# Forty modulation units ahead of the projections, forty beside them, and filter blocks in two buffers

## What is computed

```python
# first block
c_act = silu(c)
mod = c_act @ ada_w + ada_b                       # 2048 x 12288
sh1, sc1, g1, sh2, sc2, g2 = split(mod, 6)
h = rmsnorm(x, norm1_g) * (1 + sc1) + sh1
x = x + g1 * token_mixer(h, w_in, ...)            # mixers A, B, C, D: projections, attention, norm, w_out
h = rmsnorm(x, norm2_g) * (1 + sc2) + sh2
x = x + g2 * moe_ffn(h, ...)
# second block: filters, which need nothing of x
h = three layers of sin(fr * (h @ w + b)) on z;  h = (h @ w4) * decay
k = two-sided h;  k = k / sum(abs(k));  k_f = rfft(k)   # kept with hyena_bias added
```

## Time and profile before

| | |
|---|---|
| median of 3 runs | 3142.29 us (3139.79 to 3145.81) |
| the profiled execution, its own time | 3142.81 us |
| its span, first to last instruction | 3141.3 us |
| mean granted TensorE clock | 0.943 |
| PE busy | 2783.9 us (89%) |
| DVE busy | 1893.1 us (60%), 179.1 us of it in 80 modulation units (L886) |
| ACT busy | 1301.0 us (41%) |
| DMA | 645.60 MB, mean 206 GB/s; 564 loads of 1024 KB on SP's queue |

### The profile page before, as it was taken

One profiled execution on the slowest core, in us unless ns is written; L12 is line 12 of the kernel. 1 busy time (PEld: TensorE's weight loads), 2 busy tenths in 40 slices (PEclk: granted clock), 3 DMA queues, 4 the chain that ended last, 5 costly groups with the idle time before them and its releaser, 6 DMA issues.

```text
span 3141.3 us, 42584 instructions
## 1 busy us (share of the span) xinstructions
PE 2783.9 (89%) x16468; PEld 2403.4 (77%) x16468; DVE 1893.1 (60%) x2310; ACT 1301.0 (41%) x1609; POOL 32.1 (1%) x61
## 2 busy tenths in 40 slices
PE   1435999989799999999969898999898999999998
PEld 0112998877678878778759666999787998998996
DVE  7998444345666688889866544354545544545544
ACT  1001444334244457777633133444335543443443
POOL 1000000000000000000000000000000000000000
PEclk9666999889899999999989998999999999999999
DMA  9887534222077779999924333454453555455553
GB/s 368 320 342 305 179 136 161 94 81 108 18 265 248 259 273 357 358 370 375 356 78 180 139 124 132 149 186 174 147 187 141 183 187 192 180 187 189 186 186 122
DMA packets 139360, 645.60 MB, mean 206 GB/s; under 512 B 10286, under 2 KB 10361, under 8 KB 78704
## 3 DMA queue, kind: packets, MB, share of 16 engines
q1 hardware_dynamic: 130656, 593.53, 52.0%
q0 software_dynamic: 6288, 33.76, 3.0%
q10 hardware_dynamic: 2304, 16.78, 1.5%
HBM read 636.64 MB, written 7.39 MB: 205 GB/s over the span
## 4 chain that ended last, share of the span: by engine, by line
PE 73%; DVE 12%; DMA 8%; ACT 3%; issue 3%; DVEq 0%; POOL 0%; ACTq 0%; SPq 0%; POOLq 0%
PE ps L1404 72%; DMA raw<-in_stream 6%; DVE raw L886 3%; DVE w_lo L812 2%; ACT w_hi L503 1%; DMA arena<-in_hyena_bias 1%; PE ps L1487 1%; DMA filters<-arena 1%; DVE arena L942 0%; PE ps L1517 0%; DVE h_lo L861 0%; DMA arena<-in_c_row 0%; DVE arena L869 0%; DVE arena L1324 0%; DVE arena L1322 0%
## 5 line engine op out<-in xcount | busy, mean ns | idle before, releaser
L812 DVE TENSOR_TENSOR w_lo<-raw,w_hi 128x1024 fp32r<-128x1024 f32 x968 | 1171.5, 1224 | 831.7 <-ACT w_hi L503 829.0
L503 ACT ACTIVATE w_hi<-raw 128x1024 fp32r<-128x1024 f32 x968 | 1010.5, 1056 | 784.7 <-PE ps L1404 690.3
L1404 PE MATMUL ps<-h_hi,w_hi 128*128 128x256 f32 x2944 | 842.4, 286 | 26.7 <-DVE h_lo L861 14.5
L1404 PE MATMUL ps<-h_lo,w_hi 128*128 128x256 f32 x2944 | 838.5, 285 | 0.0
L1404 PE MATMUL ps<-h_hi,w_lo 128*128 128x256 f32 x2944 | 838.0, 285 | 0.0
L1404 PEld LDWEIGHTS ps<-h_hi,w_hi 128*128 128x128 f32 x2944 | 571.0, 194 | 28.5 <-issue 28.2
L1404 PEld LDWEIGHTS ps<-h_lo,w_hi 128*128 128x128 f32 x2944 | 571.1, 194 | 0.3
L1404 PEld LDWEIGHTS ps<-h_hi,w_lo 128*128 128x128 f32 x2944 | 570.6, 194 | 0.0
L1404 PE MATMUL ps<-w_hi,r_hi 128*128 128x512 f32 x1184 | 469.0, 396 | 14.4 <-DVE w_lo L812 6.9
L1404 PE MATMUL ps<-w_lo,r_hi 128*128 128x512 f32 x1184 | 462.6, 391 | 0.0
L1404 PE MATMUL ps<-w_hi,r_lo 128*128 128x512 f32 x1184 | 462.5, 391 | 0.0
(11 more groups left out here) (254 smaller groups left out, 1770.3 us busy)
## 6 DMA issues: line engine op xcount, KB each, us to landing
raw<-in_stream SPq DMA_DIRECT2D x564, 1024.0 KB, 4.9
arena<-in_mod_units ACTq DMA_DIRECT2D x16, 1024.0 KB, 4.8
filters<-arena POOLq DMA_DIRECT2D x4, 1280.0 KB, 5.6
arena<-filters POOLq DMA_DIRECT2D x4, 1280.0 KB, 6.2
arena<-in_c_row POOLq DMA_DIRECT2D x2, 1024.0 KB, 10.0
x<-in_x POOLq DMA_DIRECT2D x1, 2048.0 KB, 17.4
arena<-in_decay POOLq DMA_DIRECT2D x4, 512.0 KB, 10.5
arena<-bias_rows POOLq DMA_DIRECT2D x2, 1024.0 KB, 6.8
```

Source lines behind the costliest of these rows:

```text
L503: act.activation(dst, src, ACT.Copy).then_inc(hi_ready, 1)
L812: dve.tensor_tensor(low, src, high, ALU.subtract).then_inc(lo_ready, 1)
L1404: return pe.matmul(o, a, b, start=start, stop=stop)
```

## The change

The front keeps 40 modulation units: two behind each MLP pass, six before `norm_unit`, seven in each filter block. The 40 others are read as 80 half units of 1024 columns into two slots of their own (`aside_slot`, which with `c_row` lies in the space of `r_hi` and `r_lo`, tiles 8 to 15); DVE reduces them in steps of the projections by the table `ASIDE` (1, 1, 0 by three steps in plain phases, 2, 1, 2 beside attention, five at step 71 ahead of mixer B's attention). SP's list of loads is written out, each aside's load behind the weights of its step. Mixers C and B swap their tiles in `r_hi`, and the weights of w_out follow that order, so that tiles 8 to 15 are written last.

All four blocks' w4, decay and hyena_bias are loaded once into the space of h. Taps, absolute values, the reciprocal and the output have two buffers each. PE makes the taps of block b + 1 in two PSUM banks before the spectrum of block b, and its sums behind it; DVE evacuates the taps of block b + 1 between the parity of block b and its seven units. c_row, the MLP's weights and the DFT table are issued by ACT; POOL no longer awaits its stores one by one. The first two halves' `w_hi` and `w_lo` are made in the midst of the split of h1, and the first half of a_q, in PSUM banks 4 to 7, starts when half of h1 is split.

```diff
+FIRST_UNITS = 40
+ASIDE_HALVES = 2 * (ADA_UNITS - FIRST_UNITS)
+GAP_AT = 71
...
+        if 24 <= k < 32 or 48 <= k < 56 or 72 <= k < 80:
+            counts.append(1 if k % 3 == 1 else 2)
+        else:
+            counts.append(1 if k % 3 < 2 else 0)
+    counts[GAP_AT] += ASIDE_HALVES - sum(counts)
...
+        with nc.sbuf_tensor("under_r", [P, 2, 16 * T], F32) as under_r:
...
+        c_row = under_r[:, 0, D:2 * D]
+        aside_slot = under_r[:, 1, D:2 * D].rearrange("p (s n) -> p s n", s=2)
+        w4 = under_h[0:64, 0, :].rearrange("p (b n) -> p b n", b=4)
+        decay = under_h[:, 1, 0:2048].rearrange("p (b t n) -> p b t n", b=2, t=2)
+        hyena_b = under_h[:, 1, 2048:4096].rearrange("p (b n) -> p b n", b=4)
+        taps = [at(F_TAPS, 4, 512), under_r[:, 0, 0:D].rearrange("p (a n) -> p a n", a=4)]
+        taps_abs = [at(F_ABS, 4, 512), under_r[:, 1, 0:D].rearrange("p (a n) -> p a n", a=4)]
+        rnorm = [at(F_A, 512), at(F_RN1, 512)]
+        ko = [at(F_KO0, 5, 512), at(F_KO1, 5, 512)]
...
-            with sp.Fori(1, ADA_UNITS // SLOTS) as g:
+            with sp.Fori(1, FIRST_UNITS // SLOTS) as g:
                 for s in range(SLOTS):
...
             for s in range(SLOTS):
-                sp.wait_ge(ada_done, ADA_UNITS - 3 + s)
+                sp.wait_ge(ada_done, FIRST_UNITS - 3 + s)
                 sp.dma_start(raw[:, s, :], sp_units[ADA_UNITS + s]).then_inc(landed[s], 16)
...
-            stream(1, group_base("mix_part"))
-            for n in range(16):
...
+            def weight(n):
+
+                unit = n - BASE["mix_part"]
+                if unit >= 0:
+                    block_of, mixer = divmod(unit, 3) if unit < 12 else (unit - 12, 3)
+                    unit = 4 * block_of + (0, 2, 1, 3)[mixer]
+                sp.wait_ge(lo_ready, 2 * n - 6)
+                sp.dma_start(raw[:, n % SLOTS, :], sp_units[ADA_UNITS + BASE["mix_part"] + unit]).then_inc(landed[n % SLOTS], 16)
+
+            def aside(j):
+
+                if j >= ASIDE_HALVES:
+                    return
+                if j >= 2:
+                    sp.wait_ge(sem("aside_done"), j - 1)
+                sp.dma_start(aside_slot[:, j % 2, :], sp_units[FIRST_UNITS + j // 2][:, j % 2 * HALF:(j % 2 + 1) * HALF])\
+                    .then_inc(sem(f"aside_landed{j % 2}"), 16)
+            aside(0)
+            aside(1)
+            weight(4)
+            used = 0
+            for k in range(len(ASIDE)):
+                if k % 2 == 0:
+                    weight(k // 2 + 5)
+                for _ in range(ASIDE[k]):
+                    aside(used + 2)
+                    used += 1
+            for n in range(len(ASIDE) // 2 + 5, BASE["moe"]):
+                weight(n)
...
-            load("ld_filt", (at(F_DFT, 1280), d["dft_k"]), (at(F_ZT, T, parts=33), d["zt"]),
-                 (at(F_W1, 64, parts=33), d["filt_w1"]), (at(F_W2, 64, parts=64), d["filt_w2"]),
-                 (at(F_W3, 64, parts=64), d["filt_w3"]))
-            load("ld_c", (c_row, d["c_row"].partition_broadcast(P)))
...
+            load("ld_block", (w4, d["filt_w4"].rearrange("b p n -> p b n")),
+                 (decay.rearrange("p b t n -> p b (t n)"), d["decay"][0:2].rearrange("b p n -> p b n")),
+                 (hyena_b.rearrange("p b n -> p (b n)"), d["hyena_bias"].rearrange("b n -> (b n)").partition_broadcast(P)))
+            load("ld_narrow", (at(12960, DC, 24), d["w_gate_nsa"]))
...
-            with pool.Fori(0, 4) as b:
...
+            for b in range(4):
                 pool.wait_ge(sem("spectrum_out"), 5 * b + 5)
-                pool.dma_start(kf_dram[bass.ds(b, 1)].rearrange("a p n -> (a p) n"), at(F_KO, 2560))\
-                    .then_inc(sem("kf_stored"), 16)
-                pool.wait_ge(sem("kf_stored"), 16 * b + 16)
+                pool.dma_start(kf_dram[b], ko[b % 2].rearrange("p a n -> p (a n)")).then_inc(sem(f"kf_stored{b % 2}"), 16)
 
 
...
-            pool.wait_ge(mod_ready, ADA_UNITS // 4)
-            load("ld_narrow", (at(12960, DC, 24), d["w_gate_nsa"]))
+            pool.wait_ge(sem("kf_stored0"), 32)
+            pool.wait_ge(sem("kf_stored1"), 32)
...
-                    act.wait_ge(landed[s], 16 * (ADA_UNITS // SLOTS + 1) + 16 * (g + k // 8))
+                    act.wait_ge(landed[s], 16 * (FIRST_UNITS // SLOTS + 1) + 16 * (g + k // 8))
...
@@ -523,7 +570,12 @@
             def copy(dst, src):
                 return act.activation(dst, src, ACT.Copy)
 
-            act.wait_ge(sem("ld_c"), 16)
+            act.dma_start(c_row, d["c_row"].partition_broadcast(P)).then_inc(sem("ld_c_front"), 16)
...
@@ -550,22 +602,27 @@
                     act.wait_ge(sem("norm_rs"), norm_count(name, "rs", 1))
                     act.activation(unit[:, 0, :], src[:, 0, :], ACT.Copy, scale=stat[:, 6:7]).then_inc(sem("norm_xa"), 1)
 
-            def norm_hi(name, dst, tiles, f, first):
+            def norm_hi(name, dst, tiles, f, first, early=None):
                 for c in range(0, tiles, 4):
+                    if early and c == 8:
+                        early()
                     act.wait_ge(sem("norm_f"), norm_count(name, "f", c // 4 + 1))
                     copy(dst[:, first + c:first + c + 4, :], f[:, c:c + 4, :]).then_inc(sem("norm_hi"), 1)
 
 
             norm_root("h1", ("ld_x", 16), D, x, at(F_TAPS, TH, D), unit=x)
-            with act.Fori(0, 4) as b:
+            for b in range(4):
                 for n in range(4):
...
-                    act.activation(at(F_ABS + 512 * n, 512), at(F_TAPS + 512 * n, 512), ACT.Abs).then_inc(sem("abs_ready"), 1)
-            norm_hi("h1", h_hi, DC, hf, 0)
+                    act.activation(taps_abs[b % 2][:, n, :], taps[b % 2][:, n, :], ACT.Abs).then_inc(sem("abs_ready"), 1)
+
+            def first_hi():
+                hi(0, 0)
+                hi(0, 1)
+            norm_hi("h1", h_hi, DC, hf, 0, first_hi)
+            hi(0, 2)
             act.wait_ge(sem("ld_narrow"), 16)
             copy(n_hi[:, :, :], at(12960, DC, 24)).then_inc(sem("narrow_hi"), 1)
...
                         hi(gp, k + 3)
 
...
                             early(i, k)
                         if not (final and k + 3 >= 8 * per_iter):
                             lo(g, k + 3)
...
                     dve.tensor_tensor(dst[1][:, first + c:first + c + 4, :], f[:, c:c + 4, :],
@@ -872,22 +931,44 @@
                     if c % 4 == 3:
                         ins.then_inc(sem("norm_f"), 1)
                         dve.wait_ge(sem("norm_f"), norm_count(name, "f", c // 4 + 1))
-                        if split and c >= 7:
+                        if early and c == 7:
+                            low(0)
...
-                for s in range(SLOTS):
-                    dve.wait_ge(landed[s], 16 * g + 16)
+            def modulation(first, count):
+
+                for n in range(first, first + count):
+                    s = n % SLOTS
+                    if s == 0 and n:
+                        dve.wait_ge(mod_ready, n // 4)
+                    dve.wait_ge(landed[s], 16 * (n // SLOTS) + 16)
...
                         .then_inc(ada_done, 1)
-                dve.wait_ge(ada_done, 4 * g + 4)
-                dve.tensor_tensor(mod[:, bass.ds(4 * g, 4)], mod_sums, cols[:, bass.ds(4 * g + COLS["ada_b"], 4)], ALU.add)\
...
+                    if s == 3:
+                        dve.wait_ge(ada_done, n + 1)
+                        dve.tensor_tensor(mod[:, n - 3:n + 1], mod_sums, col("ada_b", 96)[:, n - 3:n + 1], ALU.add)\
+                            .then_inc(mod_ready, 1)
+
+            def aside(k):
+
+                for j in range(sum(ASIDE[:k]), sum(ASIDE[:k + 1])):
+                    s, u = j % 2, FIRST_UNITS + j // 2
+                    dve.wait_ge(sem(f"aside_landed{s}"), 16 * (j // 2) + 16)
+                    dve.tensor_tensor_reduce(aside_slot[:, s, :], aside_slot[:, s, :], c_row[:, s * HALF:(s + 1) * HALF], 1.0, 0.0,
+                                             ALU.mult, ALU.add, aside_sums[:, j % 8:j % 8 + 1]).then_inc(sem("aside_done"), 1)
+                    if j % 8 == 7:
+                        dve.wait_ge(sem("aside_done"), j + 1)
+                        ch(dve.tensor_tensor(mod_sums, aside_sums[:, 0:8:2], aside_sums[:, 1:8:2], ALU.add))
+                        dve.tensor_tensor(mod[:, u - 3:u + 1], mod_sums, col("ada_b", 96)[:, u - 3:u + 1], ALU.add)\
...
-                modulation(n)
-            modulation(3)
+                modulation(2 * n, 2)
+            modulation(6, 6)
...
-            with dve.Fori(0, 4) as b:
-                ch.enter(b, 2)
-                modulation(4 * b + 4)
-                dve.wait_ge(sem("ld_block"), 48 * b + 48)
+            def make_taps(b):
...
+                    ins = dve.tensor_tensor(taps[b % 2][:, n, :], ps[:, n % 2, :], decay[:, b % 2, n // 2, :], ALU.mult)
...
-                modulation(4 * b + 5)
-                dve.wait_ge(sem("taps_ready"), 4 * b + 4)
+
+            make_taps(0)
+            done_units = 12
```

(61 more changed lines are left out.)

85 lines of the change are left out of this document (42 added, 43 removed).

## The result

The changed kernel takes **3069.18 us** (median of 4 runs, 3066.30 to 3075.31) where the kernel before took 3143.91 on the same chip (3139.79 to 3145.81): ratio 0.9771, 95% interval 0.9759 to 0.9782. By this ratio the 3142.29 us from which the forecast started become 3070.3. The direction was right; 3049.7 was 20 us too low, and the time lies at the upper end of the range of 3030 to 3070, 0.3 us outside by the ratio. The profiled execution took 3068.92 us, 19.2 over the forecast. The rest of the text finds those 19.2 us.

A forecast was written before the change was run, and what follows sets the result against it. DVE was taken to bound the front up to 291 us, PE the projections from 306 us. 3142.8 - 100.9 (earlier split of h1) - 3.7 (head of a_q) + 11.5 (half units) = 3049.7 us, range 3030 to 3070.

The forecast's parts named there:

- Part 1: Front, up to the end of norm_unit: forecast to end at 58.7 us.
- with c_row at the head of ACT's own queue I take 15.5 us: Front: DVE's first MLP pass starts at 15.5 us in place of 21.5, not before 13.2.
- DVE's 37.8 us: Front: DVE's own work from its first MLP pass to norm_unit's end, with 12 units, takes 37.8 us.
- DMA makes a floor: Front: 20.0 MB of loads set norm_unit's end, at 52.2 to 60.8 us, taken as 58.7.
- Parts 2 and 3: First taps and norm take 10.0 us, the filter blocks 121.9 us, with PE hidden and no waits for loads.
- Part 4: Head of a_q: halves start 7.3 and 14.6 us after h1's split begins; gain 3.7 us.
- Part 5: The 80 half units beside projections and attention: 11.5 us lost, at least 3, at most 25.
- 0, 0.2, 1.6, 2.3, 2.5, 3.2, 4.5: Attention stretches: us by which DVE's maximum falls behind, step by step, under the table 2,1,2,2,1,2,2,1.
- 4.1 us of slack, and only 2.0 us after the last score: Attention: lag of the exponentials that PE's transposes allow; so 2.5 us lost in each of the first two stretches.
- attention pays in full: Rival, chance 0.12: each of attention's 39 halves is on the path, 44.9 us in place of 11.5, 3083 us.
- 5.0 or 4.35 us: Attention: DVE's loop through ACT per step, with or without copied heads, against a step of 5.95 us.
- Late halves: Rival, chance 0.03: DVE waits for halves' loads; landings of 9.8 us take the gain, 12 us give 3230 us.

The follow-up runs named there:

- e2: The changed kernel with the DFT table on a semaphore of its own, which PE awaits only ahead of the taps: 3068.97 us, ratio 0.9771.
- e9: The changed kernel with the filter's four small loads ahead of c_row on ACT's queue, the DFT table behind it with its own semaphore: 3066.47 us.
- e14: The changed kernel with the edits of e7 and e9, and c_row's load moved to the head of SP's queue: 3040.84 us, ratio 0.9674.
- e10: The changed kernel without pipelined filter blocks, four units reduced beside the spectrum and three beside the next norm: 3073.19 us, ratio 0.9786.
- e11: The changed kernel without pipelined filter blocks, all seven units ahead of the spectrum's evacuation: 3092.64 us, ratio 0.9836.
- e15: The changed kernel without a_q's early half: first w_hi behind all high parts of h1, w_lo behind all low parts: 3077.05 us, ratio 0.9793.
- e7: The changed kernel with halves ahead of w_lo on DVE beside attention, and their loads ahead of the step's weight on SP: 3043.69 us, ratio 0.9687.
- e1: The changed kernel with halves ahead of w_lo on DVE beside attention, SP's order kept: 3080.59 us, ratio 0.9808.
- e5: The changed kernel with one half unit in each of the 80 steps: 3083.04 us, ratio 0.9817.
- e8: The changed kernel with no half beside attention, 1,2,1 beside projections and seven in the gap: 3139.03 us, ratio 0.9994.

## Why the prediction was right in sign and 19 us off

**Part 1, wrong.** The step that failed is "with c_row at the head of ACT's own queue I take 15.5 us" for the first MLP pass. c_row did land early, and silu was done by 10.9 us; the pass hung on the whole of ACT's queue, whose last load is the DFT table, and started at 26.9. DVE's 37.8 us were right (65.03 - 26.91 = 38.1), and on this late start they, not DMA, set the end. e2 and e9, which take the table out of that wait, end at 61.9 and 60.3. That DMA makes a floor was right too: 60.7 us in e14, with 8.4 us of waits for the stream, forecast 58.7. By the limit that the Trainium skill ("DMA: Bandwidth & Descriptors", Specifications) gives for one core the forecast's estimate was 60.0; the time lies near that, the rate does not agree, since e14 averages 373 GB/s over its first 60 us, above that limit. The error of part 1 is 6.3 us at the end of norm_unit.

**Parts 2 and 3, right.** 9.99 us against 10.0, 122.6 against 121.9; PE never bound, no wait for loads. What carried the blocks' gain was not tried by the change itself. From the first MLP pass to the split it is 269.95 us before and 170.74 after, 99.2 less; 40 units at 2.30 us are 92.0 of it. By e10 pipelining gives nothing that 4 and 3 units under PE's two stages don't give; by e11 it gives 5.7 us a block against the order that leaves the norm uncovered.

**Part 4, right:** +7.5 and +14.8 us, and by e15's trace 2.7 us against 3.7.

**Part 5, wrong in size.** 23.3 us in place of 11.5. Places were right: the attention pays 20.2 of the 22.8 us up to mixer D, 2.1 follow the third, the projections almost nothing. Two steps failed. First "0, 0.2, 1.6, 2.3, 2.5, 3.2, 4.5": A's span grew by 6.0 us over the kernel before, not 4.5. Its seven steps take 6.2 to 7.3 us, none as little as PE's 5.95; they also hold waits for landings (0.94 and 0.48 us, ahead of the halves of 294.00 and 307.19) and additions (0.5 us, from 315.71 to 316.22). Second, and larger, "4.1 us of slack, and only 2.0 us after the last score" as what can be taken off the loss. PE's transposes do hide 2 us of the lag: the last ones follow the last maximum by 1.8 us, before by 3.8. But DVE itself is behind, and its own queue goes on: the last w_lo, one more half that waits for its landing, and only then the last two heads' evacuation, on which the mixer's norm hangs. The end of stretch A in the changed kernel:

```profile
331.81 0.55 PE L1630 MATMUL ps<-tab,arena 128*128 128x128 f32 x3 [3.03 <-ACT arena L665]
...
335.10 1.22 DVE L964 CUSTOM_DVE_ANT_0 under_r<-under_r 128x1024 f32<-128x1024 f32 x1 [0.76 <-DMA under_r<-in_stream]
336.25 0.16 DVE L1088 RECIPROCAL stat<-stat 128x2 f32<-128x2 f32 x1
```

Without halves that reciprocal comes 130.2 us after the split, here 138.6. The 8.4 us between them are the 7.5 us by which halves lengthen the span and 0.9 more. So each stretch pays its lag in full, where I gave only the third that treatment. The rival "attention pays in full" (each half on the path, 44.9 us) was no nearer: half of it.

What the forecast had in hand and did not use is the 2.17 and 1.51 us that DVE waits for w_hi in each step of the earlier trace rows: I counted the loop as 5.0 or 4.35 us plus the halves, without asking where in the loop they stand. Put into that wait they cost nothing (e7).

**Sum.** 6.3 us (part 1), 0.7 (blocks), 11.8 (halves), about 1 (head): 19.8, of 19.2. By the two profiles the split is 7.0 us later than forecast (197.65 against 190.6) and the way from it to the end 12.2 us longer. Of the rivals none came. Late halves did not decide in the change, but in e1, e5 and e8, and in e8 they took the whole gain, with landings of 5.2 us in the median and not the 9.8 of the forecast: the forecast let a load take 7.5 us in steps with one half every 4.3 us, and these tables ask for halves sooner than that.

What stays open is how much of a gain in the front reaches the end of the kernel. Part of what seems lost is spread between executions: from the split to mixer D's first maximum the change, e2, e9, e10 and e11 have the same code and take 406.0, 408.1, 407.9, 408.7 and 409.7 us, so the change's profile is the short one, by 2 us or more. With more than one profile of each kernel e2's gain and the part of e15's 7.9 us outside its 2.7 might be told from this spread; with these they are not.

## What to carry to other kernels

Work that is moved beside another loop costs by its place in that loop, not by its sum. Look for the wait inside the loop (here 1.7 to 2.4 us for w_hi) and put it there, and then check that the queue which feeds it does not stand behind something that this new place delays: here the first edit alone lost 11 us and both together gained 25. Two slots have a rate of their own, one load and one use per cycle (7.4 us in e8); where the table asks for more than that, time is lost while the DMA engines still have room. And a semaphore shared by several loads makes the first user wait for the last of them, here until 25.7 us for loads of 73 KB.

## What of the hardware was not expected

The queues share the DMA engines by packets, not by bytes. DMA queues of the changed kernel from 12 to 16 us (packets, MB, share of the engines' time); q0 is POOL's, q1 SP's, q10 ACT's:

```profile
q0 software_dynamic: 95, 0.78, 47.2%
q1 hardware_dynamic: 98, 0.77, 46.9%
q10 hardware_dynamic: 95, 0.12, 8.2%
```

The three queues moved as many packets each, but ACT's were of 1.3 KB on average and those of the others of 8 KB, so it got a seventh of the bytes that each of the others got. Its 713 KB behind c_row were not all there until 25.6 us, and in e9, where the 73 KB of the small loads stand ahead of c_row, c_row landed 16.6 us after its issue in place of 8.2. The Trainium skill ("DMA: Bandwidth & Descriptors", Queues, rings and completion order) has the rule: each engine takes turns between queues by the packet; these rows agree with it. The forecast reckoned by bytes alone; by packets, loads in small packets are the ones to keep away from a queue on which something urgent stands, as c_row in e9.
